# Summing the squares of queries and keys by two rounded products instead of one 32-bit product

## The chip, the core and the metric

The kernel runs on one core of a Trainium2 chip. A core has TensorE (matrix products into PSUM banks), VectorE, ScalarE, GpSimd and SyncE, each with its own instruction stream; they wait for each other on semaphores. The metric is the device time of one execution in microseconds (us); less is better.

## The reference

One decoder layer over 1024 tokens of width 1024: a SwiGLU block, a token mixer, a second SwiGLU block, a gated embedding. The change lies in the mixer, in the RMS norm of queries and keys over each head of 64 channels:

```python
proj = rms_norm(x, mix_norm) @ w_in
q, k, v, u = split(proj, ...)                 # 8 query heads, 2 key heads, 2 value heads, 512 pool channels
q = rms_norm(q.reshape(B, S, 8, 64), q_norm)  # y = x * rsqrt(mean(x*x over 64) + eps) * gain
k = rms_norm(k.reshape(B, S, 2, 64), k_norm)
a = sliding_window_attention(q, k, v, rel_bias, sinks)   # softmax over 128 keys and a sink
m = multiscale_pool(u, pool_w, pool_scale)
x = x + concat(a, m) @ w_out
```

## The kernel before

Activations stand with channels on the 128 partitions and tokens along the row. Tokens are worked in two halves of 512 (a = 0 and 1). Nearly every large product is made from rounded parts: each operand is split into a rounded part (`hi`, type float32r) and a rest (`lo`), and three products hi*hi, lo*hi and hi*lo are summed in a bank (`three`, lines 880 to 882). A projection tile of the mixer (`win`) is 8 such triples, 24 products of 128x512.

The order of work in the mixer is written out in one list, `PLAN`, made by `mix_plan`. TensorE, ScalarE and VectorE each walk this same list and do their share of each step, strictly in its order. The steps that matter here:

- ("win", a, what, i): TensorE makes a projection tile (key "k", value "v", query "q" tiles 0 to 3, pool "u"). For "k" and "q" ScalarE copies it to SBUF and at once squares it into `qb` (line 1443), which counts `qk_square`.
- ("qks", a, what, i): TensorE sums the squares over the channels of each head with one 32-bit product, `blockones` times `qb` (line 1111), into `sum_bank`. ScalarE takes the root into `qb` (line 1448), VectorE the reciprocal (line 1926), and then VectorE scales the query or key tile (line 1928). There are ten such steps.
- ("norm", 3) and ("tile", 3, k): the norm of the second token half and the splitting of its eight tiles, on VectorE (lines 1543, 1549) and ScalarE.
- ("scores", u): one round of attention, two heads of each key head over 128 queries. TensorE makes the scores (line 1131), VectorE adds bias and takes the maximum (line 1938), ScalarE the exponentials (line 1471), VectorE divides by the sum (line 1949). All of VectorE's part, its wait for ScalarE included, stands in this one step.
- ("probs", u), ("pv", u), ("pool", a, g): TensorE turns the probabilities (line 1142), multiplies them by the values (line 1090), and makes a pool product of three. GpSimd prepares the pool inputs.

In the first half of the list five `qks` steps (k and q tiles 0 to 3 of token half 0) stand between the `win` tiles. In the second half, in the first eight rounds u = 0 to 7, one `win` tile of token half 1 stands behind each `scores` step as cover for the softmax: scores(u), then in rounds 0, 3, 5, 6 and 7 a `qks` step, then the `win` tile, then pool, pv(u-1) and probs(u).

Of the kernel before, what the change touches and what calls it, by code (L numbers as in the profile page):

```python
# [9 lines left out]
F32R = mybir.dt.float32r  # L10
ACT = mybir.ActivationFunctionType
ALU = mybir.AluOpType

P = 128
# [16 lines left out]
KT = D_MODEL // P  # L31
KH = KT // 2
PT_TILES = PLE_DIM // P
HALF = SEQ // 2
# [221 lines left out]
def program(nc, xT, pT, units, gu, wd, poolw, small, const, onehot, rel, band_row, band, hl, e_dram, actc, wdc, x1, out):  # L256
    with ExitStack() as ctx:
# [7 lines left out]
        def place(name, shape, at, dt=F32):  # L265

            assert base <= at and at + size_of(shape) <= limit, (name, at, limit)
            return nc.alloc_sbuf_tensor_at(name, list(shape), dt, offset=at)

        KB = 1024  # L270
# [4 lines left out]
        extra_at = r2 + 64 * KB  # L275
# [3 lines left out]
        def keep(name, shape):  # L279
            at = misc[0]  # L280
            misc[0] += -(-size_of(shape) // 32) * 32
            return place(name, shape, at)
# [2 lines left out]
        const_sb = keep("const_sb", (P, N_CONST))  # L285
        stats = keep("stats", (P, 6, HPK))
        rel_sb = keep("rel_sb", (N_BUCKETS + 1, N_Q_HEADS))

        x_sb = place("x_sb", (P, KT, SEQ), r0)

# [10 lines left out]
        ab, bb, cb = s_at, s_at + 32 * KB, s_at + 64 * KB  # L301
# [58 lines left out]
        acc_at, rstd_at, g0_at = (r3, r3 + 4 * KB), (r3 + 2 * KB, r3 + 6 * KB), (r3 + 8 * KB, extra_at)  # L360
# [15 lines left out]
        qb_at = probs_at + 8 * KB  # L376
        assert qb_at + 2 * KB <= r2 + 40 * KB
        qb = [place("qb0", (P, HALF), qb_at), place("qb1", (P, HALF), g0_at[0])]
        pw_hi = place("pw_hi", (P, NG * P), r2 + 40 * KB, F32R)
        pw_lo = place("pw_lo", (P, NG * P), r2 + 42 * KB, F32R)  # L380
        bias = place("bias", (P, N_Q_HEADS, 2 * P), r2 + 44 * KB)
# [28 lines left out]
        blockones = const_sb[:, K_BLK:K_BLK + P]  # L410
# [8 lines left out]
        def plain(ap):  # L419

            return ap.bitcast(F32)
# [11 lines left out]
        score_bank, probsT_bank, pv_bank, sum_bank = bank[2:4], bank[4:6], bank[6], bank[7]  # L433
# [26 lines left out]
        def sem(name):  # L460
            return ctx.enter_context(nc.semaphore(name))

        small_in, const_in, oh_in, rel_in = sem("small_in"), sem("const_in"), sem("oh_in"), sem("rel_in")
# [19 lines left out]
        square_made, squares_added, sum_made = sem("square_made"), sem("squares_added"), sem("sum_made")  # L483
# [11 lines left out]
        dn_rounded, dn_split, dn_made, dp_made = sem("dn_rounded"), sem("dn_split"), sem("dn_made"), sem("dp_made")  # L495
        w2d_made, x_step, res_added = sem("w2d_made"), sem("x_step"), sem("res_added")
        qk_square, qk_sum, qk_std, qk_normed = sem("qk_square"), sem("qk_sum"), sem("qk_std"), sem("qk_normed")
        v_turned, v_copied = sem("v_turned"), sem("v_copied")
        pool_in, pool_rounded, pool_split = sem("pool_in"), sem("pool_rounded"), sem("pool_split")
        scores_made, scores_biased, max_made, exp_made = sem("scores_made"), sem("scores_biased"), sem("max_made"), sem("exp_made")  # L500
# [21 lines left out]
        def acc_count(nrm, i):  # L522

            return (KT - 1) * nrm + i
# [352 lines left out]
        def _(pe):  # L877
# [217 lines left out]
            for step in PLAN:  # L1095
                kind = step[0]
                if kind == "win":
                    n, m, a = MAIN_AT[step], MIXU_AT[step], step[1]
                    wait_main_bank(n)
                    pe.wait_ge(*unit_ready(U_MIX + m))  # L1100
                    eight(main_bank[n % 2], m % SLOTS, a, None if a in seen else 2 + a).then_inc(main_made, 1)
                    seen.add(a)
                elif kind == "norm":
                    if step[1] == 3:
                        norm_sum(3)
                elif kind == "qks":

                    i = QKS_AT[step[1:]]
                    pe.wait_ge(qk_square, i + 1)
                    wait_sum_bank(step)  # L1110
                    pe.matmul(sum_bank[:, :], blockones, qb[i % 2][:, :], start=True, stop=True).then_inc(qk_sum, 1)
                elif kind == "vt":
                    pe.wait_ge(main_copied, copied(("win", step[1], "v", 0)))
                    wait_sum_bank(step)
                    for j in range(HB):
                        c = slice(j * P, (j + 1) * P)
                        last = pe.transpose(sum_bank[:, c], vT[:, c], ident)
                    last.then_inc(v_turned, 1)
                elif kind == "scores":
                    u = step[1]  # L1120
                    b, off = u // 2, (P if u < 2 else 0)
                    if u == 0:
                        pe.wait_ge(res_added, RES_FFN)
                    pe.wait_ge(qk_normed, QKS_AT[(b // HB, "q", HPK - 1)] + 1)
                    if u:
                        pe.wait_ge(scores_biased, HPK * u)

                    for j in (0, 2, 1, 3):
                        kv, h = round_head(u, j)
                        p0, c = kv * HEAD_DIM, (j % 2) * 2 * P  # L1130
                        last = pe.matmul(score_bank[j // 2][:, c + off:c + 2 * P],  # L1131
                                         q_sb[p0:p0 + HEAD_DIM, h, b * P:(b + 1) * P],
                                         k_sb[p0:p0 + HEAD_DIM, max(b - 1, 0) * P:(b + 1) * P], start=True, stop=True)
                    last.then_inc(scores_made, 1)
                elif kind == "probs":
                    u = step[1]
                    pe.wait_ge(probs_normed, HPK * (u + 1))
                    if u:
                        pe.wait_ge(probsT_copied, u)
                    for kb in ((1,) if u < 2 else (0, 1)):  # L1140
                        for h in range(HPK):
                            last = pe.transpose(probsT_bank[kb][:, h * P:(h + 1) * P],  # L1142
                                                probs[:, h, kb * P:(kb + 1) * P], ident)
                    last.then_inc(probs_turned, 1)
                elif kind == "pv":
                    if step[1] < 2 * NB - 1:
                        pv(step[1])
                elif kind == "pool":
                    n, g = MAIN_AT[step], step[2]
                    wait_main_bank(n)  # L1150
                    pe.wait_ge(poolw_split, 1)
                    pe.wait_ge(pool_in, POOLS.index(step[1:]) + 1)
                    c = slice(g * P, (g + 1) * P)
                    three(main_bank[n % 2][:, :], pw_hi[:, c], pw_lo[:, c], d_hi[:, :], d_lo[:, :],
                          True, True).then_inc(main_made, 1)
                elif kind == "wouts":

                    pe.wait_ge(pool_split, NG * 2)
                    for d in (0, 1):
                        wout = ("wout", 1, d)  # L1160
                        n, m = MAIN_AT[wout], MIXU_AT[wout]
                        wait_main_bank(n)
                        pe.wait_ge(*unit_ready(U_MIX + m))
                        terms(main_bank[n % 2], m % SLOTS, 1, range(HPK, KT), stop=False)
                        if d == 0:
                            pv(2 * NB - 1)
                    norm_sum(4)
                elif kind == "wout":
                    n, m, a = MAIN_AT[step], MIXU_AT[step], step[1]
                    pe.wait_ge(attn_split, NB * (a + 1))  # L1170
                    if a and step[2] < 2:
                        terms(main_bank[n % 2], m % SLOTS, a, range(HPK), start=False).then_inc(main_made, 1)
                        continue
                    wait_main_bank(n)
                    pe.wait_ge(*unit_ready(U_MIX + m))
                    pe.wait_ge(pool_split, NG * (a + 1))
                    eight(main_bank[n % 2], m % SLOTS, a).then_inc(main_made, 1)
# [14 lines left out]
        def _(act):  # L1192
# [36 lines left out]
            def round_first(ph, n):  # L1229

                q, b = n // 4, n % 4
                act.wait_ge(gu_in[q % 2], 16 * (ph * QUADS // 2 + q // 2 + 1))
                act.activation(t_hi[t_slot(n)][:, :], weight_block(q, b), ACT.Copy).then_inc(t_rounded, 1)
# [168 lines left out]
            for n in range(2, 2 * KT):  # L1402
# [8 lines left out]
                elif n >= KT:  # L1411
                    round_s(0, "h", 0, n - KT)
            round_first(0, 3)
            act.wait_ge(band_made, 1)
            act.activation(gband[:, :], band_bank[0:N_Q_HEADS, 0:SKEW], ACT.Copy).then_inc(band_copied, 1)
            for k in range(KT):
# [99 lines left out]
        def _(dve):  # L1516
# [392 lines left out]
            for step in PLAN:  # L1909
# [12 lines left out]
                elif kind == "qks":  # L1922
                    a, what, i = step[1:]
                    j = QKS_AT[step[1:]]
                    dve.wait_ge(qk_std, j + 1)
                    link(dve.reciprocal(qb[j % 2][:, :], qb[j % 2][:, :]))  # L1926
                    t = k_sb[:, tok(a)] if what == "k" else q_sb[:, i, tok(a)]
# [165 lines left out]
```

## Time and profile before

| | us |
|---|---|
| median of 3 runs | 1685.7 |
| lowest, highest | 1685.17, 1686.51 |
| the profiled execution | 1685.31 |
| its span, first to last instruction | 1683.5 |
| TensorE busy | 1654.2 (98%) |
| VectorE busy | 1198.4 (71%) |
| ScalarE busy | 677.4 (40%) |
| GpSimd busy | 295.3 (18%) |

A row of the timeline gives the start in us from the span's beginning, the length in us, the engine (PE is TensorE, DVE is VectorE, ACT is ScalarE, POOL is GpSimd), the line of the kernel, and output<-inputs; in brackets, the idle time just before and what ended it. Products overlap: the length of one is longer than the distance to the next start, and it is the distance that counts.

### The profile page before, as it was taken

The numbers are of one execution on the slowest core, as the hardware profiler recorded it, in microseconds if no ns is written. First come the engines' busy times: TensorE is split into PE (matmuls) and PEld (weight loads), VectorE is DVE, ScalarE is ACT, GpSimd is POOL, SyncE is SP. The second block draws the span as 40 slices with busy tenths as digits, with TensorE's granted clock in tenths as the row PEclk, the third lists the DMA queues.
The fourth block names the chain that finished last, engine by engine and source line by source line (L and its number), as shares of the span: only waits on it lengthen the run. The fifth ranks groups of instructions, "written<-read, shape, count | busy, mean of one in ns | idle before, by whom it ended". The sixth has DMA issues, their size and how long they took to land.

```text
span 1683.5 us, 20491 instructions
## 1 busy us (share of the span) xinstructions
PE 1654.2 (98%) x7378; PEld 1346.1 (80%) x7378; DVE 1198.4 (71%) x1736; ACT 677.4 (40%) x1095; POOL 295.3 (18%) x333
## 2 busy tenths in 40 slices
PE   7989999999999999998999999999999999999998
PEld 5878888888888887776777888888888888888887
DVE  6988887877755778576665698777766764666763
ACT  7533343333344445245644343333322334434431
POOL 0022332433100000034140003323343200000000
PEclk9999999999999999999999999999999999999999
DMA  9148777777679765343345406677455349876465
GB/s 320 38 175 315 281 276 269 268 272 254 228 231 360 234 194 169 117 164 121 100 152 196 153 23 218 242 256 265 185 188 200 120 160 327 289 252 190 152 218 175
DMA packets 135241, 351.12 MB, mean 209 GB/s; under 512 B 12604, under 2 KB 54245, under 8 KB 126821
## 3 DMA queue, kind: packets, MB, share of 16 engines
q1 hardware_dynamic: 119160, 297.59, 51.4%
q0 software_dynamic: 12672, 46.14, 7.8%
q10 hardware_dynamic: 3308, 6.08, 1.0%
q8 instruction: 59, 0.97, 0.2%
q14 instruction: 42, 0.34, 0.1%
HBM read 245.42 MB, written 105.92 MB: 209 GB/s over the span
## 4 chain that ended last, share of the span: by engine, by line
PE 84%; DVE 6%; ACT 2%; DMA 1%; issue 1%; SPq 0%; ACTq 0%; DVEq 0%
PE bank L880 27%; PE bank L882 27%; PE bank L881 27%; ACT probs L1471 1%; DVE probs L1938 1%; DVE qb L1926 1%; DVE probs L1949 1%; PE bank L1142 1%; PE bank L1131 1%; DVE dn_lo L1760 1%; PE bank L1090 0%; DMA e_acc<-e_dram 0%; DMA d_f<-wdc 0%; ACT dn_hi L1281 0%; DVE hn L1543 0%
## 5 line engine op out<-in xcount | busy, mean ns | idle before, releaser
L880 PE MATMUL bank<-h_hi,t_hi 128*128 128x512 f32 x704 | 275.0, 391 | 2.9 <-ACT p L1264 2.9
L1760 DVE TENSOR_TENSOR dn_lo<-d_f,dn_hi 128x1024 fp32r<-128x1024 f32 x154 | 185.2, 1221 | 125.3 <-ACT dn_hi L1281 124.9
L882 PE MATMUL bank<-h_hi,t_lo 128*128 128x512 f32 x704 | 274.0, 389 | 0.0
L881 PE MATMUL bank<-h_lo,t_hi 128*128 128x512 f32 x704 | 274.0, 389 | 0.0
L880 PE MATMUL bank<-dn_hi 128*128 128x512 f32 x616 | 241.4, 392 | 1.1 <-DVE dn_lo L1760 1.0
L881 PE MATMUL bank<-dn_lo,dn_hi 128*128 128x512 f32 x616 | 239.8, 389 | 0.0
L882 PE MATMUL bank<-dn_hi,dn_lo 128*128 128x512 f32 x616 | 239.8, 389 | 0.0
L1281 ACT ACTIVATE dn_hi<-d_f 128x1024 fp32r<-128x1024 f32 x154 | 160.3, 1056 | 162.2 <-DMA d_f<-in_wd 86.5
L861 POOL TENSOR_TENSOR wdr<-wdr 128x256 f32<-128x256 f32 x176 | 174.4, 991 | 245.2 <-DMA wdr<-in_wd 234.8
L880 PE MATMUL bank<-c_hi,t_hi 128*128 128x512 f32 x544 | 212.2, 390 | 2.4 <-DVE c L1622 2.4
L881 PE MATMUL bank<-c_lo,t_hi 128*128 128x512 f32 x544 | 212.4, 390 | 0.0
L882 PE MATMUL bank<-c_hi,t_lo 128*128 128x512 f32 x544 | 212.4, 390 | 0.0
L880 PE MATMUL bank<-h_hi,w_hi 128*128 128x512 f32 x416 | 168.9, 406 | 0.0
L882 PE MATMUL bank<-h_hi,w_lo 128*128 128x512 f32 x416 | 162.2, 390 | 0.0
L881 PE MATMUL bank<-h_lo,w_hi 128*128 128x512 f32 x416 | 162.2, 390 | 0.0
L880 PEld LDWEIGHTS bank<-h_hi,t_hi 128*128 128x128 f32 x704 | 132.3, 188 | 31.7 <-issue 4.4
L881 PEld LDWEIGHTS bank<-h_lo,t_hi 128*128 128x128 f32 x704 | 132.2, 188 | 27.8 <-issue 0.5
L882 PEld LDWEIGHTS bank<-h_hi,t_lo 128*128 128x128 f32 x704 | 132.2, 188 | 27.5
L1246 ACT ACTIVATE t_hi<-t_f 128x512 fp32r<-128x512 f32 x160 | 96.4, 626 | 130.3 <-DVE t_f L1586 124.4
L880 PEld LDWEIGHTS bank<-dn_hi 128*128 128x128 f32 x616 | 115.6, 188 | 27.2 <-DVE dn_lo L1760 2.6
L881 PEld LDWEIGHTS bank<-dn_lo,dn_hi 128*128 128x128 f32 x616 | 115.7, 188 | 24.7 <-issue 0.7
L882 PEld LDWEIGHTS bank<-dn_hi,dn_lo 128*128 128x128 f32 x616 | 115.6, 188 | 24.0
(159 smaller groups left out, 2391.4 us busy)
## 6 DMA issues: line engine op xcount, KB each, us to landing
raw<-in_gu SPq DMA_DIRECT2D x44, 1024.0 KB, 5.3
d_f<-actc SPq DMA_DIRECT2D x154, 256.0 KB, 3.5
actc<-acts SPq DMA_DIRECT2D x20, 1792.0 KB, 6.8
w_hi<-hl SPq DMA_DIRECT2D x52, 512.0 KB, 4.2
w_lo<-hl SPq DMA_DIRECT2D x52, 512.0 KB, 5.3
wdr<-in_wd POOLq DMA_DIRECT2D x44, 512.0 KB, 4.9
wdc<-wdr POOLq DMA_DIRECT2D x44, 512.0 KB, 3.5
d_f<-wdc SPq DMA_DIRECT2D x88, 256.0 KB, 3.3
```

Of the source, the lines that this page charges most:

```text
L861: pool.tensor_tensor(blocks[to], blocks[one], blocks[two], ALU.add).then_inc(wd_made, 1)
L880: pe.matmul(ps, whi, vhi, start=first, stop=False, skip_group_check=onto)
L881: pe.matmul(ps, whi, vlo, start=False, stop=False, skip_group_check=onto)
L882: return pe.matmul(ps, wlo, vhi, start=False, stop=last, skip_group_check=onto)
L1131: last = pe.matmul(score_bank[j // 2][:, c + off:c + 2 * P], q_sb[p0:p0 + HEAD_DIM, h, b * P:(b + 1) * P], k_sb[p0:p0 + HEAD_DIM, max(b - ...
L1142: last = pe.transpose(probsT_bank[kb][:, h * P:(h + 1) * P], probs[:, h, kb * P:(kb + 1) * P], ident)
L1246: act.activation(t_hi[i][:, :], src, ACT.Copy).then_inc(t_rounded, 1)
L1281: act.activation(dn_hi[slot][:, :], d_f[slot][:, :], ACT.Copy).then_inc(dn_rounded, 1)
L1471: last = act.activation(probs[:, h, off:], probs[:, h, off:], ACT.Exp, bias=stats[:, NEGM, h:h + 1], accum_out=stats[:, DEN, h:h + 1])
L1760: dve.tensor_tensor(dn_lo[slot][:, :], d_f[slot][:, :], plain(dn_hi[slot][:, :]), ALU.subtract).then_inc(dn_split, 1)
L1926: link(dve.reciprocal(qb[j % 2][:, :], qb[j % 2][:, :]))
L1938: dve.tensor_tensor_reduce(probs[:, h, off:], score_bank[h // 2][:, c + off:c + 2 * P], bias[:, hh, off:], 1.0, col(C_SINK + hh), ALU.add, ...
```

## The change

Ahead of each sum VectorE splits the squares: a rounded copy `qb_hi`, and the rest `qb_lo`, which takes the place of `qb` in memory. TensorE then sums both parts with two float32r products against `block_r`, a float32r copy of the 0/1 matrix that ScalarE makes once near the start of the program. TensorE waits for the split (`qk_split`) where it waited for the squares (`qk_square`). VectorE makes the split in its share of the `qks` step. `qb_hi` lies where the squares of the norm (`sq`) lie, so that the first split also waits for the last of those sums.

```diff
+        block_r = place("block_r", (P, P), extra_at + 2 * KB, F32R)
...
+        qb_lo = [place("qb_lo0", (P, HALF), qb_at, F32R), place("qb_lo1", (P, HALF), g0_at[0], F32R)]
+        qb_hi = [place(f"qb_hi{i}", (P, HALF), cb + 40 * KB + 2 * KB * i, F32R) for i in (0, 1)]
...
@@ TensorE, step "qks"
-                    pe.wait_ge(qk_square, i + 1)
+                    pe.wait_ge(block_made, 1)
+                    pe.wait_ge(qk_split, i + 1)
                     wait_sum_bank(step)
-                    pe.matmul(sum_bank[:, :], blockones, qb[i % 2][:, :], start=True, stop=True).then_inc(qk_sum, 1)
+                    pe.matmul(sum_bank[:, :], block_r[:, :], qb_hi[i % 2][:, :], start=True, stop=False)
+                    pe.matmul(sum_bank[:, :], block_r[:, :], qb_lo[i % 2][:, :], start=False, stop=True).then_inc(qk_sum, 1)
@@ ScalarE, near the start
+            act.wait_ge(const_in, 16)
+            act.activation(block_r[:, :], blockones, ACT.Copy).then_inc(block_made, 1)
@@ VectorE, step "qks"
+                    dve.wait_ge(qk_square, j + 1)
+                    if j == 0:
+                        dve.wait_ge(squares_added, acc_count(3, KT - 1))
+                    if j >= 2:
+                        dve.wait_ge(qk_sum, j - 1)
+                    dve.tensor_copy(qb_hi[j % 2][:, :], qb[j % 2][:, :]).then_inc(qk_rounded, 1)
+                    dve.wait_ge(qk_rounded, j + 1)
+                    dve.tensor_tensor(qb_lo[j % 2][:, :], qb[j % 2][:, :], plain(qb_hi[j % 2][:, :]), ALU.subtract).then_inc(qk_split, 1)
                     dve.wait_ge(qk_std, j + 1)
```

TensorE in round 3 of the attention, before: the last of the score products, the sum, and the first product of the `win` tile behind it.

```order
L1131 MATMUL bank<-k_sb,q_sb 128x256 [waits scores_biased,qk_normed]
L1131 MATMUL bank<-k_sb,q_sb 128x256 x3
L1111 MATMUL bank<-qb_154,const_sb 128x512 [waits v_copied,qk_square]
L880 MATMUL bank<-h_hi_63,w_hi_72 128x512 [waits w_in2,main_copied]
L881 MATMUL bank<-h_lo_65,w_hi_72 128x512
```

The same place in the changed kernel, whose line numbers are a few higher:

```order
L1137 MATMUL bank<-k_sb,q_sb 128x256 [waits scores_biased,qk_normed]
L1137 MATMUL bank<-k_sb,q_sb 128x256 x3
L1116 MATMUL bank<-qb_hi_159,block_r 128x512 [waits v_copied,qk_split,block_made]
L1117 MATMUL bank<-qb_lo_157,block_r 128x512
L884 MATMUL bank<-h_hi_64,w_hi_73 128x512 [waits w_in2,main_copied]
```

One product became two, the wait is for the split, and the `win` tile still stands behind it.

VectorE in the same round, before: ISA rows are line 1938 with its reading of the maximum; `qb` is the buffer of the squares.

```order
L1938 ISA probs,stats<-bank,bias,small_sb 128x256
L1938 ISA stats 128x1
L1942 TENSOR_SCALAR stats<-stats 128x4 [waits scores_biased]
L1944 TENSOR_TENSOR stats<-stats,small_sb 128x4 [waits dve_step]
L1946 TENSOR_TENSOR stats<-stats 128x4 [waits exp_made]
L1947 RECIPROCAL stats<-stats 128x4 [waits dve_step]
L1949 TENSOR_SCALAR probs<-probs,stats 128x256 [waits dve_step]
L1949 TENSOR_SCALAR probs<-probs,stats 128x256 x3
L1926 RECIPROCAL qb_154<-qb_154 128x512 [waits qk_std]
L1928 SCALAR_TENSOR_TENSOR q_sb<-q_sb,small_sb,qb_154 128x512 [waits dve_step]
```

And in the changed kernel:

```order
L1959 TENSOR_SCALAR stats<-stats 128x4 [waits scores_biased]
L1961 TENSOR_TENSOR stats<-stats,small_sb 128x4 [waits dve_step]
L1963 TENSOR_TENSOR stats<-stats 128x4 [waits exp_made]
L1964 RECIPROCAL stats<-stats 128x4 [waits dve_step]
L1966 TENSOR_SCALAR probs<-probs,stats 128x256 [waits dve_step]
L1966 TENSOR_SCALAR probs<-probs,stats 128x256 x3
L1939 CAST qb_hi_159<-qb_155 128x512 [waits qk_sum,qk_square]
L1941 TENSOR_TENSOR qb_lo_157<-qb_155,qb_hi_159 128x512 [waits qk_rounded]
L1943 RECIPROCAL qb_155<-qb_155 128x512 [waits qk_std]
L1945 SCALAR_TENSOR_TENSOR q_sb<-q_sb,small_sb,qb_155 128x512 [waits dve_step]
```

The two new operations stand behind the whole softmax of the round and ahead of the reciprocal.

VectorE in the first half of the list, from the norm's reciprocal on, before:

```order
L1536 RECIPROCAL rstd_143<-rstd_143 128x512 [waits std_made]
L1926 RECIPROCAL qb_155<-qb_155 128x512 [waits qk_std]
L1928 SCALAR_TENSOR_TENSOR q_sb<-q_sb,small_sb,qb_155 128x512 [waits dve_step]
L1926 RECIPROCAL qb_154<-qb_154 128x512 [waits qk_std]
L1928 SCALAR_TENSOR_TENSOR q_sb<-q_sb,small_sb,qb_154 128x512 [waits dve_step]
```

And in the changed kernel:

```order
L1544 RECIPROCAL rstd_144<-rstd_144 128x512 [waits std_made]
L1939 CAST qb_hi_160<-qb_156 128x512 [waits qk_square,rstd_made]
L1941 TENSOR_TENSOR qb_lo_158<-qb_156,qb_hi_160 128x512 [waits qk_rounded]
L1943 RECIPROCAL qb_156<-qb_156 128x512 [waits qk_std]
L1945 SCALAR_TENSOR_TENSOR q_sb<-q_sb,small_sb,qb_156 128x512 [waits dve_step]
L1939 CAST qb_hi_159<-qb_155 128x512 [waits qk_sum,qk_square]
L1941 TENSOR_TENSOR qb_lo_157<-qb_155,qb_hi_159 128x512 [waits qk_rounded]
L1943 RECIPROCAL qb_155<-qb_155 128x512 [waits qk_std]
L1945 SCALAR_TENSOR_TENSOR q_sb<-q_sb,small_sb,qb_155 128x512 [waits dve_step]
```

Here each split stands behind the scaling of the tile before it.

## Rows read from the trace of the kernel before

**Rows 1.** The page: busy time by engine; the chain's shares by engine.

```profile
PE 1654.2 (98%) x7378; PEld 1346.1 (80%) x7378; DVE 1198.4 (71%) x1736; ACT 677.4 (40%) x1095; POOL 295.3 (18%) x333
...
PE 84%; DVE 6%; ACT 2%; DMA 1%; issue 1%; SPq 0%; ACTq 0%; DVEq 0%
```

**Rows 2.** Waits of TensorE, whole span: us in total, times, longest us.

```profile
PE bank L1142 <- DVE probs L1949: 7.4, 6, 2.8
```

**Rows 3.** Timeline of TensorE, first half: start, us, line, operation, idle before.

```profile
692.70 1.02 PE L1111 MATMUL bank<-qb,const_sb 128*128 128x512 f32 x2
...
705.39 1.02 PE L1111 MATMUL bank<-qb,const_sb 128*128 128x512 f32 x2
...
711.51 0.39 PE L882 MATMUL bank<-h_hi,w_lo 128*128 128x512 f32 x1
711.74 1.02 PE L1111 MATMUL bank<-qb,const_sb 128*128 128x512 f32 x2
```

**Rows 4.** Timeline of VectorE over the same stretch.

```profile
701.11 3.35 DVE L1536 RECIPROCAL rstd<-rstd 128x512 f32<-128x512 f32 x1 [2.39 <-ACT rstd L1212]
...
710.91 0.75 DVE L1928 SCALAR_TENSOR_TENSOR q_sb<-q_sb,small_sb,qb 128x512 f32<-128x512 f32 x1
...
717.86 0.75 DVE L1543 SCALAR_TENSOR_TENSOR hn<-x_sb,small_sb,rstd 128x512 f32<-128x512 f32 x1
...
725.75 0.69 DVE L1549 TENSOR_TENSOR h_lo<-hn,h_hi 128x512 fp32r<-128x512 f32 x1
```

**Rows 5.** Timeline of ScalarE: the key's square, and the roots behind two sums.

```profile
688.09 0.63 ACT L1443 ACTIVATE qb<-k_sb 128x512 f32<-128x512 f32 x1
...
693.76 0.69 ACT L1448 ACTIVATE qb<-bank,small_sb 128x512 f32<-128x512 f32 x1 [0.26 <-PE bank L1111]
...
706.75 0.67 ACT L1448 ACTIVATE qb<-bank,small_sb 128x512 f32<-128x512 f32 x1
```

**Rows 6.** Timeline of VectorE at the start: a cast and a subtraction of 1024 columns.

```profile
6.26 0.69 DVE L1878 CAST p_hi<-p_raw 128x1024 fp32r<-128x1024 f32 x1 [5.40 <-DMA p_raw<-in_pT]
6.99 1.22 DVE L1880 TENSOR_TENSOR p_lo<-p_raw,p_hi 128x1024 fp32r<-128x1024 f32 x1
```

**Rows 7.** Timeline of TensorE in the attention rounds, without its `win` tiles.

```profile
747.66 0.72 PE L1131 MATMUL bank<-k_sb,q_sb 64*128 64x128 f32 x8
749.08 1.12 PE L1111 MATMUL bank<-qb,const_sb 128*128 128x512 f32 x2 [0.70 <-ACT qb L1443]
...
775.21 1.14 PE L1131 MATMUL bank<-k_sb,q_sb 64*128 64x256 f32 x8
...
796.28 1.09 PE L1142 MATMUL bank<-const_sb,probs 128*128 128x128 f32 x8 [2.76 <-DVE probs L1949]
797.30 1.14 PE L1131 MATMUL bank<-k_sb,q_sb 64*128 64x256 f32 x8
798.37 1.12 PE L1111 MATMUL bank<-qb,const_sb 128*128 128x512 f32 x2
...
851.82 1.09 PE L1142 MATMUL bank<-const_sb,probs 128*128 128x128 f32 x8 [0.77 <-DVE probs L1949]
...
870.86 1.09 PE L1142 MATMUL bank<-const_sb,probs 128*128 128x128 f32 x8 [0.73 <-DVE probs L1949]
```

**Rows 8.** Timeline of VectorE in rounds 0, 3 and 5.

```profile
752.53 0.87 DVE L1949 TENSOR_SCALAR probs<-probs,stats 128x128 f32<-128x128 f32 x4
...
781.27 2.68 DVE L1949 TENSOR_SCALAR probs<-probs,stats 128x256 f32<-128x256 f32 x4
...
798.48 0.48 DVE L1938 CUSTOM_DVE_ANT_0 probs<-bank,bias,small_sb 128x256 f32<-128x256 f32 x1 [1.27 <-PE bank L1131]
...
803.24 1.14 DVE L1949 TENSOR_SCALAR probs<-probs,stats 128x256 f32<-128x256 f32 x4
```

**Rows 9.** Timeline of TensorE from its first product on.

```profile
9.50 0.76 PE L880 MATMUL bank<-p_hi,pj_hi 128*128 128x512 f32 x1 [9.50 <-DVE pj_lo L1884]
...
13.44 0.39 PE L880 MATMUL bank<-p_hi,pj_hi 128*128 128x512 f32 x1
```

More of the change, by code:

```diff
@@ L497, in program @@
         qk_square, qk_sum, qk_std, qk_normed = sem("qk_square"), sem("qk_sum"), sem("qk_std"), sem("qk_normed")
+        block_made, qk_rounded, qk_split = sem("block_made"), sem("qk_rounded"), sem("qk_split")
         v_turned, v_copied = sem("v_turned"), sem("v_copied")
```

## The prediction, made before the changed kernel was run

> **What bounds the kernel now.** First the busy times: TensorE is busy 98% of the span and carries 84% of the chain that ended last [rows 1]. So a microsecond taken from TensorE's stream is a microsecond of the result, and so is one in which TensorE is made to wait, since nothing later has slack to absorb it. Then TensorE's waits: in the whole mixer it waits mainly for VectorE's probabilities, 7.4 us in six waits [rows 2]. Then the timelines of TensorE, VectorE and ScalarE around the ten sums. In the first half TensorE does not wait: the sums follow at 6.35 us (705.39, 711.74) [rows 3]. In the attention rounds it starts the sum as soon as the scores are made (797.30, 798.37) [rows 7] while VectorE needs until 804.38 for the softmax of that round [rows 8]. The squares come from ScalarE, which is early; VectorE, which is late, comes into it only behind the sum. That is what the change turns round.
>
> **What TensorE saves.** The sum is two records, as a plain 32-bit product is made in more than one pass. From one sum to the next are 6.35 us, of which the 24 products of the `win` tile take 24 x 0.227 = 5.44 (0.23 between 711.51 and 711.74) [rows 3]; 0.91 is left for the sum. Two float32r products cost 2 x 0.227 = 0.45. The saving is 0.455 a sum, **4.5 us** for ten. Below it is subtracted where each sum stands. The copy of the 0/1 matrix on ScalarE is one small operation 680 us ahead of its use and costs nothing; were its cover gone, it would be under the 0.69 of a ScalarE operation of 512 columns [rows 5].
>
> **What the split takes.** The cast of 1024 columns took 0.69 and the subtraction 1.22 [rows 6]. A subtraction of 512 took 0.69 [rows 4], so that a part of some 0.16 does not shrink; a cast of 512 is then between 0.34 and 0.69, and I take 0.43. With 0.04 between the two and 0.06 until TensorE starts, a split is ready **1.22 us** after VectorE turns to it. What counts is when it turns to it.
>
> **First half, five sums.** The key's sum: its square is made at 688.09 + 0.63 [rows 5] and VectorE has nothing else to do, so the split is ready by 690, and TensorE comes only at 692.70 [rows 3]. No wait, and all after it 0.45 earlier. First query sum: TensorE comes at 705.39 - 0.45 = 704.94. VectorE is at the norm's reciprocal until 701.11 + 3.35 - 0.45 = 704.01 [rows 4]; plus 1.22 is 705.23: wait 0.3. From then on there is a loop through all three engines: the sum (record 0.62, then 0.04; the first root stood 0.04 behind the record's end, 692.70 + 1.02 against 693.76 [rows 3, 5]), root 0.67 to 0.69, reciprocal 3.35, scaling 0.7, the next split 1.22. That is 6.65. At the first query sum ScalarE is still squaring the next tile when the sum is made: the root stood 1.36 behind the sum's start (705.39, 706.75) instead of 1.06 [rows 3, 5], and with the shorter sum it is 0.4 late. So the second query's split is ready 7.05 behind the first query's sum. For the third and fourth VectorE has a tile of the norm in between (0.7 for its scaling, then 0.7 more for a split of the tile before [rows 4]): 7.4 and 8.0. TensorE's own work between two sums is 5.44 + 0.45 = 5.89. So it waits 1.2, 1.5 and 2.1. Waits 5.1 us, saved 5 x 0.455 = 2.3: **+2.8 us**. The tiles of the norm that VectorE makes afterwards end some 1.5 us later, TensorE comes 2.8 later, so no new wait there.
>
> **Attention rounds, five sums.** VectorE's share of a `scores` step ends with the division, and the split stands behind it (see the order above). Round 5: scores start at 797.30, division ends at 803.24 + 1.14 = 804.38 [rows 7, 8], 7.08 behind; plus 1.22, the sum can start 8.30 after the scores instead of 1.07: 7.23 more. Rounds 6 and 7 have the same pieces: from the first biasing operation (798.48) to the end of the division are 5.90 [rows 8], and I take 7.23 for each. Round 3: division ends at 781.27 + 2.68 = 783.95, 8.74 behind 775.21 [rows 7, 8], since GpSimd is at work beside it and will be again; 9.96 - 1.06 = 8.90. Round 0, narrower: 752.53 + 0.87 = 753.40, 5.74 behind 747.66, plus 1.22 is 6.96 against 1.42 before: 5.54 more. Sum 36.1. Queued behind TensorE's wait is the `win` tile, which is the cover of the softmax: it now runs when there is nothing left to cover. What the cover is freed of: of the 7.4 us of waiting for the probabilities, 0.77 and 0.73 are in later rounds [rows 2, 7], and 5.9 are in rounds 1, 3, 4 and 7. They come from VectorE being late with a reciprocal and a scaling that now fall under the `win` tile (or, in round 4, from the late start that these caused), and go: -5.9. Saved on sums: -2.3. **+27.9 us**. VectorE's reciprocal and scaling then end some 14 us after the scores' start, TensorE's next scores come after 16 or more, so there is no second wait.
>
> **TensorE's clock.** After its first idle time of 9.50 us TensorE made nine products in 3.94 us (9.50 to 13.44), 0.43 apart instead of 0.227: the lower of its two levels, 1.2 and 2.4 GHz, though the granted clock reads 1.00 [rows 9]. After an idle time of 2.76 the next starts are at full pace (796.28, 797.30, 798.37) [rows 7]. The new idle times are 6.3, 8.9, 7.2, 7.2 and 7.2 us, nearer to the first, so I take its price for each: 3.94 - 9 x 0.227 = 1.9, in all **+9.5 us**. The first half's waits of 0.3 to 2.1 are under 2.76 and cost nothing more.
>
> The Trainium skill has a rule for this ("TensorE: Matmul & The Clock Gate", the section "HAM oscillation — how this bites in real kernels"): a kernel that waits for microseconds between bursts of products loses the full clock at each wait and starts each burst slow. Rows 9 agree, on the one long idle time there is. By the rule the sum is +40.2, without it +30.7.
>
> **Sum.** 2.8 + 27.9 + 9.5 = +40.2 us on the profiled execution's 1685.3, that is 1725.5. The median is 0.4 higher: **1726 us**, 1.024 times the time before.
>
> **The rivals.** *The clock stays up.* All waits come, the products behind them run at full pace: 1685.7 + 30.7 = 1716. For it: the only idle time that did cost the clock is longer than any new one and lies before the first product. Against it: 7 to 9 us is far from the 2.76 that cost nothing. *The clock stays down longer.* The slow stretch behind a wait lasts for the whole sum and `win` tile, 5.89 us of work at half pace, so 5.9 lost each time and not 1.9: 1726 + 5 x 4.0 = 1746. Rows 9 speak against it, but they are one sample. *The split is in time (the other side).* If VectorE had the halves ready when TensorE comes, the change would give its 4.5 us: 1681. It decides at the point where VectorE turns to the split 1.22 us or more before TensorE comes. Where squares are made long before, VectorE would have idle time for it, but the order puts each split behind the softmax or behind the tile before, and only the first key sum meets the condition. *Waits are moved, not added.* If the new waits at the sum were only the old waits at the probabilities come earlier, +0 to +5 would be left: 1686 to 1691. Against it: the old ones are 5.9 in all where the new ones are 36, and the `win` tile of 5.44 cannot start before.
>
> **How the numbers follow.** Forecast 0.65 (1720 to 1733, for casts of 0.34 to 0.69 and a slow stretch from half to twice as costly); clock stays up 0.20 (1711 to 1720); clock down longer 0.09 (1733 to 1746); waits moved 0.03; split in time 0.03. The range of 1712 to 1734 holds the first two and a little of the third. A measurement can tell about 0.2% (3.4 us) from no change: faster 0.03, same 0.02, slower 0.95.
>
> **What would show it.** TensorE's waits in the changed kernel should name VectorE's subtraction into `qb_lo` as what ended them: four in the first half (0.3, 1.2, 1.5, 2.1) and five in the rounds (6.3, 8.9, 7.2, 7.2, 7.2), and the waits at line 1142's successor should shrink from 7.4 to about 1.5. Distances of 0.43 between products behind the long waits show the clock, 0.23 refute it. The cast's row should read about 0.43. I would be wrong if the sums start right behind the scores, if ScalarE's table of functions for the root is loaded behind the sum instead of during the wait, or if something behind the rounds turns out to have slack.

## The result and the profile after

| | before | after |
|---|---|---|
| median of 3 runs, us | 1685.7 | 1727.02 |
| lowest, highest | 1685.17, 1686.51 | 1726.0, 1729.22 |
| span of the profiled execution | 1683.5 | 1727.4 |

The changed kernel is slower: ratio 1.0246, 95% interval 1.0227 to 1.0264. The forecast was 1726.

The page of the changed kernel: busy times by engine, and the granted clock in 40 slices (tenths of full speed). Compare [rows 1].

```profile
PE 1662.0 (96%) x7378; PEld 1353.5 (78%) x7378; DVE 1203.8 (70%) x1756; ACT 678.4 (39%) x1096; POOL 291.4 (17%) x333
...
PEclk9999999999999999988799999999999999999999
```

TensorE has as many instructions as before, two products for a sum as there were two records, and is idle for 36 us more (span less busy: 29.3 before, 65.4 after). The granted clock falls in the slices 18 to 20, which are the attention rounds. TensorE's waits in the changed kernel (line, what ended them: us in total, times, longest); the fellow of the second row is [rows 2]:

```profile
PE bank L1116 <- issue: 41.4, 9, 8.7
PE bank L1148 <- DVE probs L1966: 2.2, 3, 0.8
```

Line 1116 is the first product of the sum. The page puts these waits down to "issue". In the run with fillers below, where TensorE waits for the split last, behind the wait for the bank, the waits at the same nine sums are put down to VectorE's subtraction into `qb_lo`; four of them (0.25, 0.83, 1.30, 1.90) are those of the first half, where nothing but this order is changed. So the name hangs on how the waits are put in the program; by what rule was not tried. Timeline of TensorE in the changed kernel, the sums of the first half and around the five of the attention rounds; it answers [rows 3, 7]:

```profile
705.87 0.47 PE L1116 MATMUL bank<-qb_hi,block_r 128*128 128x512 f32 x1 [0.20 <-issue]
712.88 0.47 PE L1116 MATMUL bank<-qb_hi,block_r 128*128 128x512 f32 x1 [0.83 <-issue]
720.30 0.47 PE L1116 MATMUL bank<-qb_hi,block_r 128*128 128x512 f32 x1 [1.26 <-issue]
728.33 0.47 PE L1116 MATMUL bank<-qb_hi,block_r 128*128 128x512 f32 x1 [1.85 <-issue]
...
751.25 0.72 PE L1137 MATMUL bank<-k_sb,q_sb 64*128 64x128 f32 x8
758.14 0.76 PE L1116 MATMUL bank<-qb_hi,block_r 128*128 128x512 f32 x1 [6.18 <-issue]
795.72 0.77 PE L1116 MATMUL bank<-qb_hi,block_r 128*128 128x512 f32 x1 [8.73 <-issue]
816.10 1.13 PE L1137 MATMUL bank<-k_sb,q_sb 64*128 64x256 f32 x8
824.93 0.76 PE L1116 MATMUL bank<-qb_hi,block_r 128*128 128x512 f32 x1 [7.70 <-issue]
843.17 0.76 PE L1116 MATMUL bank<-qb_hi,block_r 128*128 128x512 f32 x1 [7.11 <-issue]
861.98 0.77 PE L1116 MATMUL bank<-qb_hi,block_r 128*128 128x512 f32 x1 [7.51 <-issue]
878.74 1.14 PE L1137 MATMUL bank<-k_sb,q_sb 64*128 64x256 f32 x8
```

Four waits in the first half, five in the rounds. The last row is the start of round 8. Before, it was here:

```profile
834.93 1.14 PE L1131 MATMUL bank<-k_sb,q_sb 64*128 64x256 f32 x8
```

So all but 0.1 us of the difference of the spans, 43.9, has come up by then (43.8). VectorE in round 5 of the changed kernel shows why; it answers [rows 8]:

```profile
817.28 0.48 DVE L1955 CUSTOM_DVE_ANT_0 probs<-bank,bias,small_sb 128x256 f32<-128x256 f32 x1 [0.83 <-PE bank L1137]
...
819.02 0.77 DVE L1959 TENSOR_SCALAR stats<-stats 128x4 f32<-128x4 f32 x1
...
822.22 0.16 DVE L1963 TENSOR_TENSOR stats<-stats 128x4 f32<-128x4 f32 x1 [2.24 <-ACT probs L1479]
...
822.63 1.14 DVE L1966 TENSOR_SCALAR probs<-probs,stats 128x256 f32<-128x256 f32 x4
823.69 0.42 DVE L1939 CAST qb_hi<-qb 128x512 fp32r<-128x512 f32 x1
824.14 0.69 DVE L1941 TENSOR_TENSOR qb_lo<-qb,qb_hi 128x512 fp32r<-128x512 f32 x1
826.88 3.35 DVE L1943 RECIPROCAL qb<-qb 128x512 f32<-128x512 f32 x1 [2.05 <-ACT qb L1456]
```

The split ends at 824.83, and TensorE starts the sum at 824.93, 8.83 behind the scores at 816.10. The split itself is 1.14 us; the 6.4 ahead of it are the softmax. The row at 819.02 took 0.17 in the same round before (line 1942 there); now GpSimd is at work beside it.

### The profile page after: what moved, and what is told of

It reads as the page before. It is cut to its first block, busy times and chain, and to the rows that moved or that the text cites. A ratio compares the mean times of both kernels' runs of the same rounds, so it can differ in the third digit from the quotient of the medians.

```text
span 1727.4 us, 20520 instructions
## 1 busy us (share of the span) xinstructions
PE 1662.0 (96%) x7378; PEld 1353.5 (78%) x7378; DVE 1203.8 (70%) x1756; ACT 678.4 (39%) x1096; POOL 291.4 (17%) x333
## 4 chain that ended last, share of the span: by engine, by line
PE 86%; DVE 4%; issue 3%; ACT 1%; DMA 1%; SPq 0%; ACTq 0%; DVEq 0%
PE bank L884 28%; PE bank L885 27%; PE bank L886 27%; PE bank L1137 1%; PE bank L1148 1%; PE bank L1094 1%; DVE dn_lo L1768 1%; DMA e_acc<-e_dram 0%; ACT probs L1479 0%; DMA d_f<-wdc 0%; ACT dn_hi L1287 0%; DVE probs L1955 0%; PE bank L1116 0%; DVE probs L1966 0%; DVE hn L1551 0%
## 5 line engine op out<-in xcount | busy, mean ns | idle before, releaser
L865 POOL TENSOR_TENSOR wdr<-wdr 128x256 f32<-128x256 f32 x176 | 170.9, 971 | 242.7 <-DMA wdr<-in_wd 232.3
```

The costliest lines, as they stand in the source:

```text
L865: pool.tensor_tensor(blocks[to], blocks[one], blocks[two], ALU.add).then_inc(wd_made, 1)
```

## The experiments

**Only the first half.** The five sums of the attention rounds go back to the plain product, without a split.

```diff
-                    pe.wait_ge(qk_split, i + 1)
...
+                    if i < 5:
+                        ...two rounded products behind qk_split, as in the changed kernel
+                    else:
+                        pe.wait_ge(qk_square, i + 1)
+                        wait_sum_bank(step)
+                        pe.matmul(sum_bank[:, :], blockones, qb[i % 2][:, :], start=True, stop=True).then_inc(qk_sum, 1)
```

> The split and the two rounded products in the five sums of the first half only; the five sums of the attention rounds are made as before, by one plain product of the unsplit squares. Theory (the time is lost where the split stands behind a round's softmax): only the first half's share is left, 3 us over before, 1689. Rival (each split costs about the same wherever it stands, 41/10 us): 1685.7 + 20 = 1706.

Measured: 1689.01, before on the same chip 1684.59, ratio 1.0027 (1.0017 to 1.0038), so 4.4 more where 3 was expected; its profiled execution's span is 3.0 above that of before. The rival's 1706 is refuted. The loss is not shared out evenly over ten sums: about 37 of 41 us come in the rounds.

**The products alone.** Two rounded products of one rounded tile, no split.

```diff
-                        act.activation(qb[j % 2][:, :], dst, ACT.Square).then_inc(qk_square, 1)
+                        act.activation(qb_lo[j % 2][:, :], dst, ACT.Square).then_inc(qk_square, 1)
...
-                    pe.wait_ge(qk_split, i + 1)
+                    pe.wait_ge(qk_square, i + 1)
...
-                    pe.matmul(sum_bank[:, :], block_r[:, :], qb_hi[i % 2][:, :], start=True, stop=False)
+                    pe.matmul(sum_bank[:, :], block_r[:, :], qb_lo[i % 2][:, :], start=True, stop=False)
```

> The two rounded products without the split: ScalarE writes the squares rounded, and both products read this one tile, so that the sum is doubled and the rest part is left out of the computation. TensorE waits for the squares, as before. Theory: the products themselves save 0.455 each, 4.5 us in all: 1681. Rival (two rounded products cost what one 32-bit product costs): 1685.7.

Measured: 1680.83 against 1684.59, ratio 0.998 (0.997 to 0.9989): 3.8 us less. That two rounded products are cheaper than the plain one holds, at about the size forecast.

**The waits with the plain product.** Splits and waits as in the changed kernel, and the plain product of `qb_hi` behind them.

```diff
-                    pe.matmul(sum_bank[:, :], block_r[:, :], qb_hi[i % 2][:, :], start=True, stop=False)
-                    pe.matmul(sum_bank[:, :], block_r[:, :], qb_lo[i % 2][:, :], start=False, stop=True).then_inc(qk_sum, 1)
+                    pe.matmul(sum_bank[:, :], blockones, plain(qb_hi[i % 2][:, :]), start=True, stop=True).then_inc(qk_sum, 1)
```

> The changed kernel with its splits and its waits, but the sum made by one plain 32-bit product of the rounded part alone; the rest part is left out of the sum. Theory: the product's 0.455 comes back ten times, 4.5 us over the changed kernel, and a little more where it runs at the lower clock: 1727 + 4.5 to 7 = 1732 to 1734. Rival (with the waits there the products' cost is hidden): 1727.

Measured: 1730.96 against 1685.05, ratio 1.0277 (1.0263 to 1.0291), 3.9 above the changed kernel's 1727.02, a little under what was expected. Each taken against the kernel before on its own chip (1685.05 and 1685.7), it is 4.6 above. With the run above it separates the two parts: the products give some 4 us with the waits or without, the waits and what follows from them take some 45.

**Fillers.** While TensorE waits in a round it makes products that nobody reads. The wait for the bank goes ahead of them.

```diff
                     pe.wait_ge(block_made, 1)
+                    wait_sum_bank(step)
+                    if i >= 5:
+                        pe.wait_ge(poolw_split, 1)
+                        for _ in range((22, 34, 28, 26, 28)[i - 5]):
+                            pe.matmul(sum_bank[:, :], block_r[:, :], pw_hi[:, :], start=True, stop=True)
                     pe.wait_ge(qk_split, i + 1)
-                    wait_sum_bank(step)
```

> The changed kernel, and in the five attention rounds TensorE makes 22, 34, 28, 26 and 28 products of 128x512 into the sum's bank, read by nobody, while it waits for the split; all of its real work starts no earlier. Theory (the products behind a long wait run at the lower of the two clock levels): sums and win tiles behind the waits run 0.23 apart, and the 11.9 us that they took longer go: 1715. Rival (they are slow for another reason, or the waits alone make the 41 us): 1727.

Measured: 1717.15 against 1684.59, ratio 1.0193 (1.0178 to 1.0208): 9.9 under the changed kernel, 8.8 when each is taken against before on its own chip. First TensorE in round 5 of the changed kernel, the sum and the products behind the wait:

```profile
824.93 0.76 PE L1116 MATMUL bank<-qb_hi,block_r 128*128 128x512 f32 x1 [7.70 <-issue]
825.50 0.63 PE L1117 MATMUL bank<-qb_lo,block_r 128*128 128x512 f32 x1
825.92 0.63 PE L884 MATMUL bank<-h_hi,w_hi 128*128 128x512 f32 x1
826.35 0.63 PE L885 MATMUL bank<-h_lo,w_hi 128*128 128x512 f32 x1
...
828.91 0.43 PE L885 MATMUL bank<-h_lo,w_hi 128*128 128x512 f32 x1
829.17 0.40 PE L886 MATMUL bank<-h_hi,w_lo 128*128 128x512 f32 x1
829.41 0.39 PE L884 MATMUL bank<-h_hi,w_hi 128*128 128x512 f32 x1
...
832.90 1.08 PE L1094 MATMUL bank<-probsT,v_sb 128*64 128x256 f32 x8
```

The starts are 0.43 apart until 828.91 and 0.23 from 829.17 on: the 1.2 GHz level for 4 us, then 2.4 GHz. And the same round with the fillers (line 1118; the sum is at lines 1120 and 1121 there):

```profile
811.28 6.64 PE L1118 MATMUL bank<-pw_hi,block_r 128*128 128x512 f32 x28
819.04 0.50 PE L1120 MATMUL bank<-qb_hi,block_r 128*128 128x512 f32 x1 [1.12 <-DVE qb_lo L1945]
...
825.20 1.08 PE L1094 MATMUL bank<-probsT,v_sb 128*64 128x256 f32 x8
```

From the sum's start to the value products are 6.16 us, where the changed kernel took 7.97. Over the five rounds the same difference is 2.76, 2.76, 1.81, 1.30 and 2.11, together 10.7 us (1.3 to 2.8 a wait; the 11.9 of the expectation was read against an ideal pace). The granted clock, in one window over the rounds of each kernel, changed first and fillers second (the columns are the window, its length, busy times of PE, PEld, DVE, ACT, POOL, then the granted clock, DMA share and GB/s):

```profile
750.00:870.00 120.00, 82.05 (x376) 61.41 (x374) 62.22 (x158) 52.00 (x123) 27.32 (x32) 0.83 0.21 72
```

```profile
750.00:860.00 110.00, 104.58 (x521) 79.18 (x519) 62.30 (x158) 52.63 (x124) 27.38 (x32) 1.00 0.23 78
```

The idle time costs the clock, and keeping TensorE at work gives it back. In the first half of this execution eight products ran at 0.43, behind a wait of 1.90 at the sum at 726.44, as they did not in the changed kernel's profile. From the first sum to the scores of round 0 are 59.73 us here and 58.00 there; these 1.7 take the 10.7 to 9.0, about the 8.8 of the medians. The other 32.6 us over the kernel before stay, the waits themselves for the most part.

**The split inside the softmax.** In the rounds VectorE makes the split before it waits for the exponentials.

```diff
                     dve.tensor_tensor(stats[:, SM, :], stats[:, NEGM, :], small_sb[:, c:c + HPK], ALU.add).then_inc(max_made, 1)
+                    if u in (0, 3, 5, 6, 7):
+                        split_squares(5 + (0, 3, 5, 6, 7).index(u))
                     dve.wait_ge(exp_made, u + 1)
```

> In the attention rounds VectorE makes the split between the maximum and its wait for the exponentials, where it is idle for 2.2 us; the first half as in the changed kernel. Theory: the split is ready 4.5 us after the scores' start instead of 8.3, TensorE waits about 3.4 in rounds 3, 5, 6, 7 and 2.8 in round 0, the softmax ends no later. 3.0 (first half) + 4 x 3.4 + 2.1 - 5.9 (old waits covered) - 2.3 (products) = +10.5: 1696 if waits of 3.4 us do not cost the clock; up to 10 more, 1706, if they do. Rival (what costs is the two more operations on VectorE, not their place): 1727.

Measured: 1709.21 against 1684.59, ratio 1.0145 (1.0129 to 1.016). The same two operations some 4 us earlier in VectorE's stream take 18 us off, so that their place costs, and not only their time: the rival's 1727 is refuted. It is above the 1706 of the expectation: the waits were 2.80, 5.27, 3.92, 3.33 and 4.79, 20.1 us and not 16.4, and the granted clock over 750 to 860 is 0.89, so that these shorter waits cost the clock too (in this execution the first half has a fall as well, at 727.68). In rounds 3 and 7 the split now falls beside GpSimd's work; round 7:

```profile
840.59 1.50 DVE L1920 CAST qb_hi<-qb 128x512 fp32r<-128x512 f32 x1
840.53 1.27 POOL L845 TENSOR_TENSOR win_b<-win_b,ub 128x512 f32<-128x512 f32 x1
```

The cast took 1.50 there and 1.29 in round 3, and 0.42 in round 5, where GpSimd was done before it; the subtraction of round 3 took 1.65 instead of 0.69. TensorE in this kernel in round 0, behind a wait of 2.80:

```profile
754.44 0.47 PE L1116 MATMUL bank<-qb_hi,block_r 128*128 128x512 f32 x1 [2.80 <-issue]
754.75 0.50 PE L1117 MATMUL bank<-qb_lo,block_r 128*128 128x512 f32 x1
755.05 0.63 PE L884 MATMUL bank<-h_hi,w_hi 128*128 128x512 f32 x1
755.48 0.63 PE L885 MATMUL bank<-h_lo,w_hi 128*128 128x512 f32 x1
```

The sum still starts at full pace, the tile behind it is 0.43 apart.

**All splits forward.** VectorE makes each split in the step in which ScalarE makes the squares.

```diff
+                if kind == "win" and step[2] in ("k", "q"):
+                    split_squares(QKS_AT[step[1:]])
...
-                    (the split in the "qks" step)
```

> All ten splits moved forward on VectorE, to its share of the win step in which ScalarE makes the squares, everything else as in the changed kernel. Theory: the halves are ready before TensorE comes, except for the key of token half 1 (round 0), where the square itself is late and the split adds 1.2 us: 1685.7 - 4.5 + 1.2 = 1682.4. Rival (VectorE has no room for 12 us more of work in the mixer, wherever it stands): waits for the probabilities grow, 1686 or more.

Measured: 1690.84 against 1685.05, ratio 1.0037 (1.0025 to 1.005). My theory was 8 us too low. The first half is as expected, without a wait. The wait at the key's sum in round 0 is 1.94, as expected (0.7 before, and 1.2 for the split). But the waits at the sums of rounds 6 and 7 are back, 2.48 and 3.36. Behind the longer one, which ends at 822.51, the products stand 0.43 apart for 5 us, some 2.5 us more. VectorE in this kernel, end of round 5 and start of round 6; its scores stand at 805.57 on TensorE:

```profile
803.88 3.35 DVE L1947 RECIPROCAL qb<-qb 128x512 f32<-128x512 f32 x1 [0.45 <-ACT qb L1456]
807.27 0.75 DVE L1949 SCALAR_TENSOR_TENSOR q_sb<-q_sb,small_sb,qb 128x512 f32<-128x512 f32 x1
807.94 0.42 DVE L1920 CAST qb_hi<-qb 128x512 fp32r<-128x512 f32 x1
808.39 0.69 DVE L1922 TENSOR_TENSOR qb_lo<-qb,qb_hi 128x512 fp32r<-128x512 f32 x1
809.00 0.42 DVE L1976 TENSOR_TENSOR h_lo<-bank,h_hi 128x256 fp32r<-128x256 f32 x1
809.34 0.47 DVE L1959 CUSTOM_DVE_ANT_0 probs<-bank,bias,small_sb 128x256 f32<-128x256 f32 x1
```

The squares were ready at 805.0, but ahead of the split stand the softmax, the reciprocal and the scaling of the query tile before. The first biasing operation of round 5 was at 797.54, that of round 6 is at 809.34: VectorE's round is 11.8 us long where TensorE's was 9.6 (797.30 to 806.92 before). In the kernel before VectorE's round was 10.7 already (798.48 to 809.22), and two rounds later TensorE waited 1.47 for the probabilities. In three rounds in a row with a sum VectorE is the bound, and a split made earlier is still a split more. The rival was right that VectorE lacks room, though the wait shows at the sums and not at the probabilities.

**One sum moved by a round,** with all splits forward, and as a control in the kernel before.

```diff
-    ready = {0: [("qks", 1, "k", 0)], 1: [("vt", 1)], 3: [("qks", 1, "q", 0)], 5: [("qks", 1, "q", 1)],
+    ready = {1: [("qks", 1, "k", 0), ("vt", 1)], 3: [("qks", 1, "q", 0)], 5: [("qks", 1, "q", 1)],
```

> The run above, and the sum of the key of token half 1 moved from round 0 to round 1, where its split has long been ready. Theory: the last wait goes as well, 0.7 that were there before and the 1.2 of the split: 1680.5. Rival: VectorE is later in round 1 and hands the wait to the probabilities: 1682 to 1684.

> The kernel before with that one move of a sum from round 0 to round 1, no split. Theory: the wait of 0.7 at the sum in round 0 goes, and the wait of 1.5 in round 1 becomes none or moves to round 2: 1684 to 1685.7. So most of the gain of the run above over before is the products' 4.5. Rival: the move itself makes the gain: 1681.

Measured: 1694.67 and 1691.48 against 1685.05, ratios 1.0058 (1.0046 to 1.0071) and 1.004 (1.0027 to 1.0052). Both theory and rival were wrong. TensorE in the control, rounds 1 and 4:

```profile
753.73 1.12 PE L1111 MATMUL bank<-qb,const_sb 128*128 128x512 f32 x2
760.44 1.09 PE L1117 MATMUL bank<-const_sb,vT 128*128 128x128 f32 x4 [5.59 <-ACT qb L1448]
...
800.68 1.97 PE L1142 MATMUL bank<-const_sb,probs 128*128 128x128 f32 x8 [2.77 <-DVE probs L1949]
```

The sum and the turning of the values (`vt`) share one bank. ScalarE reads the sum out of it only behind the exponentials of the round, which end at 758.2, and the loading of its table (1.28):

```profile
759.61 0.69 ACT L1448 ACTIVATE qb<-bank,small_sb 128x512 f32<-128x512 f32 x1
```

The turning waits 5.6 us for that, and in the control the products behind it stand 0.43 apart for some 5 us. The move put two users of the bank side by side; in the run with the splits forward the same wait is 5.64.

**First half forward, rounds plain.** Where VectorE has room the split is made, forward; in the rounds the plain product stays.

```diff
-                if kind == "win" and step[2] in ("k", "q"):
+                if kind == "win" and step[2] in ("k", "q") and QKS_AT[step[1:]] < 5:
```

> Split and rounded products in the first half only, the split at the win step as in the run with all ten moved forward; the five sums of the attention rounds are made by the plain product without a split. Theory (moved forward, the split costs nothing where VectorE has room, and it has room in the first half; the loss of the all-early run lies in the rounds): five savings of 0.455 and no wait: 1685.0 - 2.3 = 1682.8. Rival (the early split delays VectorE in the first half too and is paid for later): 1685 or more.

Measured: 1682.49 (11 runs) against 1685.22 (21 runs), ratio 0.9983 (0.9974 to 0.9992). No wait at a sum of the first half is left, as the theory had it. This is the one version that computes the whole layer and is faster than the kernel before, by 2.7 us (1.3 to 4.4 by the interval).

**The split off VectorE.** The run above, and in rounds 3, 5, 6 and 7 ScalarE and GpSimd make the split.

```diff
+                        if j > 5:
+                            act.activation(qb_hi[j % 2][:, :], dst, ACT.Square)
                         act.activation(qb[j % 2][:, :], dst, ACT.Square).then_inc(qk_square, 1)
...
+                elif step[0] == "win" and step[1] == 1 and step[2] == "q":
+                    j = QKS_AT[step[1:]]
+                    pool.wait_ge(qk_square, j + 1)
+                    pool.tensor_tensor(qb_lo[j % 2][:, :], qb[j % 2][:, :], plain(qb_hi[j % 2][:, :]), ALU.subtract).then_inc(qk_rest, 1)
```

> The run above, and for the four query sums of the attention rounds the split is made off VectorE: ScalarE writes the square twice, once rounded, and GpSimd subtracts; the key's sum in round 0 stays plain. Theory (in rounds 5 to 7 the limit is VectorE's row of softmax, reciprocal, scaling and split, 11.8 us against TensorE's 10): with the split off VectorE four more savings come in, 1682.8 - 1.8 = 1681.0. Rival (GpSimd's subtraction of about 1.3 us or ScalarE's extra 0.6 delay the round as much as VectorE's split did): waits at the sum in rounds 6 and 7, 1685 to 1690.

Measured: 1686.33 against 1685.22, ratio 1.0008 (0.9999 to 1.0017), no gain: the theory's 1681.0 was wrong, and the time lies where the rival had it. TensorE's waits in the mixer of this kernel:

```profile
PE bank L1157 <- DVE probs L1981: 9.2, 8, 3.7
PE bank L1121 <- issue: 1.3, 1, 1.3
```

The waits at the split sums are gone but for one of 1.3. Those at the probabilities grew from 7.5 in the run above to 9.2, one of them to 3.7, and behind that one the products run at the lower clock again. GpSimd's pool work now starts later and runs beside other parts of the softmax: in round 7 the division took 2.46 beside it (1.14 in the run above), and one small operation ahead of the exponentials 1.15 (0.16 there). These 2.3 us are about what that wait grew by, from 1.48 to 3.66. A run without GpSimd's work beside the softmax was not made, nor one with the sum placed behind the `win` tile on TensorE.

## Why the prediction was right

**The sum on TensorE.** Forecast 4.5 us for the products; runs gave 3.8 and 3.9 (4.6 against before on its own chip). Right.

**The split.** Forecast 0.43 for the cast, 1.22 in all. The cast took 0.42 (411 to 426 ns over ten), the subtraction 0.69, and from VectorE's turn to TensorE's start in round 5 are 1.24 (823.69 to 824.93). Right, and the estimate from the 1024-column rows [rows 6] was close.

**First half.** Forecast waits 0.3, 1.2, 1.5, 2.1; the rows read 0.20, 0.83, 1.26, 1.85, counted from the end of the record before. In starts, round 0 is 3.59 later than before, of which 0.55 were there at the first sum already: 3.0 against the forecast 2.8.

**Attention rounds.** Forecast waits 6.3, 8.9, 7.2, 7.2, 7.2; measured 6.18, 8.73, 7.70, 7.11, 7.51. Round 8 starts 43.81 later, less 3.59 and less the clock's 10.7 is 29.5, against 27.9. The step that was too hopeful: of the old waits at the probabilities all four of rounds 1, 3, 4 and 7 were to go, 5.9 us. One of 0.73 stayed in round 1, and 5.2 went (7.4 less 2.2). Most of the rest is in rounds 5 and 7, whose sums start 8.83 and 8.64 behind the scores where 8.30 was forecast: a small operation of the softmax took 0.77 and 0.57 there instead of 0.17, beside GpSimd's work. I had named such overlap only for round 3, and taken rounds 5 to 7 as alike. ScalarE loaded its table for the root during the wait, as counted on (822.21 to 823.49 in round 5).

**The clock.** Forecast 1.9 a wait, 9.5; measured 10.7 by the difference to the fillers, 1.3 to 2.8 a wait. The mechanism is shown, the term was small by an eighth, and the even price hid a spread of two to one. (The granted clock of 1.00 over 9.50 to 13.44 stands in the trace before, though not in rows 9.) What does not hold is the line that I drew at 2.76 us. In the control and in the run with only the first half changed the same wait at the probabilities of round 4 was followed by transposes at half pace, 1.97 where the kernel before had 1.09:

```profile
797.70 1.97 PE L1153 MATMUL bank<-const_sb,probs 128*128 128x128 f32 x8 [2.76 <-DVE probs L1972]
```

So a wait of 2.76 or 2.77 us cost the clock in two of the profiled runs and cost nothing in five. All waits of 2.80 and more in the rounds were followed by products at the lower level, at once or some 0.6 us later. But the length of the one wait does not decide it either. Near 114 us the changed kernel has a wait of 3.29 with products at full pace behind it, and in the runs with fillers and with the split inside the softmax eight products fell to 0.43 behind a wait of 1.9 in the first half. The kernel before, too, has a fall that I overlooked, behind waits of 2.85 and 2.39:

```profile
121.60 0.47 PE L880 MATMUL bank<-c_hi,t_hi 128*128 128x512 f32 x1 [2.39 <-DVE c L1622]
...
122.99 0.63 PE L882 MATMUL bank<-c_hi,t_lo 128*128 128x512 f32 x1
123.41 0.63 PE L880 MATMUL bank<-c_hi,t_hi 128*128 128x512 f32 x1
```

What decides in a given execution stays open; that the first half's waits cost no clock in the changed kernel's profile holds for that execution and not for those two others.

**The rivals.** The clock stays up: refuted by the fillers. What I put down for it, that no idle time behind the first product cost the clock, was misread: the fall at 122.59 in the kernel before spoke against it. The clock stays down longer: the slow stretch is 3 to 6 us, at most 14 of the 26 products, nowhere the whole tile at half pace. The split in time: true of one sum in ten, as the order said. Waits moved, not added: 5.2 of 41.

**Sum.** 40.2 forecast on the profiled execution. Its span grew 43.9, the medians 41.3. The three terms were each low, by 3.6 us together (0.8, of which 0.55 stood there before the first sum, 1.6 and 1.2). That the median came within 1.0 of the forecast is in part luck: the profiled execution of the changed kernel was the longest of its three, 2.2 above their median, while that of before was 0.4 below its own. What I said would name the waits was wrong: the profile has "issue" there.

## What to carry to other kernels

When a wait is moved from a fast producer to another engine, read what stands ahead of the new producer's work in its own stream: two operations of together 1.1 us, made ten times, cost 41 us here, because they stood behind a softmax, in front of the very tile that covered it. Put such a preparation right behind its input, and only where that engine has room for it; where the engine is already the bound of the stretch, the cheaper product on another engine is worth less than the preparation it asks for. Ask also what a third engine does at the new place: beside GpSimd's work the same cast took three times as long. And beside the wait itself, count some 2 us for the clock of TensorE behind each wait of about 3 us or more, and look for such falls behind shorter ones (1.9 us in two runs here).

## What the runs showed of the hardware

In the attention rounds every wait of TensorE of 2.80 us or more was followed by products at the 1.2 GHz level (0.43 apart), one of 2.76 or 2.77 in two runs of seven; elsewhere a wait of 1.90 was (the fillers), and one of 3.29 was not (the changed kernel, 113.96). Each fall in the rounds of the changed kernel cost 1.3 to 2.8 us. That agrees with the Trainium skill ("TensorE: Matmul & The Clock Gate", the section "HAM oscillation — how this bites in real kernels"), by which each burst behind a wait of microseconds starts slow, for the long waits of the changed kernel. It does not hold for every wait: behind those of 2.80 and 3.92 us in the run with the split inside the softmax the sum still ran at full pace and the products fell to 0.43 some 0.6 us later, and behind the 3.29 named above they did not fall at once. The fillers show the other side of it, that products which nobody reads keep the clock.

Beside work of GpSimd a cast of 128x512 on VectorE took 1.29 and 1.50 us instead of 0.42, a subtraction of 128x512 1.65 instead of 0.69 (the run with the split inside the softmax), and a division of four tiles of 128x256 2.46 instead of 1.14 (the split off VectorE).

The plain 32-bit product of 128x512 costs as much as four rounded ones (0.91 against 0.227 each, by the distances in the first half of the kernel before), so that two products of a split operand take half its time on TensorE where the other operand, being 0 and 1, needs no rest part.
